# A float32 two-block transformer on one core: head biases on VectorE, the last projection and norm by tokens, finished tiles ahead of weight splits, shorter lags in the convolution stages

## The reference

```
sc = where(allowed, q.k * scale - slope[h] * |i - j|, -inf)      # 8 differential heads, two softmaxes each
z  = q.k * scale                                                  # 8 stick-breaking heads
sc = where(valid, q.k * scale + rel_table[h, clip(i - j)], -inf)  # 8 heads of a band of chunks
x  = x + y @ w_o
g  = causal_dwconv(rmsnorm(x) @ w_gate);  u = rmsnorm(x) @ w_up
x  = x + (silu(g) * u) @ w_down
out = x * rsqrt(mean(x * x) + 1e-6) * final_norm
```

## Time and profile before

| | |
|---|---|
| median of three runs | 2740.82 us |
| profiled execution, its own time | 2740.66 us |
| its span | 2738.8 us |
| TensorE busy / VectorE / ScalarE / GpSimd | 99% / 72% / 47% / 3% |
| DMA: read and written, mean rate, share of its queue for the weights | 499 MB, 182 GB/s, 54.8% |
| weight split on ScalarE / on VectorE, mean | 1.056 / 1.234 us, 929 each |
| chain that ended last, TensorE's share | 95% |

### The profile page before, as it was taken

How to read it: one execution, slowest core, us unless ns; L and a number is a source line. 1 busy time by engine, 2 the same in 40 slices (tenths; PEclk the granted TensorE clock), 3 DMA queues, 4 the chain that set the end, 5 groups by cost and what they waited for, 6 DMA issues and landing times.

```text
span 2738.8 us, 38092 instructions
## 1 busy us (share of the span) xinstructions
PE 2711.5 (99%) x15646; PEld 2356.6 (86%) x15646; DVE 1960.4 (72%) x2399; ACT 1291.2 (47%) x1648; POOL 95.0 (3%) x69
## 2 busy tenths in 40 slices
PE   8999999999999999999999999999999999999997
PEld 7888888888898888888888888888888888888886
DVE  7777888876768665666566885776787757775775
ACT  5444456754545443444344554545544433443444
POOL 1000000011101000000000110000100000000001
PEclk9999999999999999999999999999999999999999
DMA  6555554446555556555555555454555655565553
GB/s 240 191 185 185 178 169 168 145 160 223 181 169 191 186 190 195 191 189 190 192 184 192 193 182 172 148 168 143 166 184 185 201 191 178 196 196 190 185 194 123
DMA packets 138189, 499.01 MB, mean 182 GB/s; under 512 B 15248, under 2 KB 16280, under 8 KB 137888
## 3 DMA queue, kind: packets, MB, share of 16 engines
q1 hardware_dynamic: 136224, 491.67, 54.8%
q10 hardware_dynamic: 1792, 4.91, 0.5%
HBM read 494.41 MB, written 2.11 MB: 181 GB/s over the span
## 4 chain that ended last, share of the span: by engine, by line
PE 95%; DVE 3%; ACT 1%; issue 0%; POOL 0%; DMA 0%; DVEq 0%; ACTq 0%; POOLq 0%
PE PS L484 95%; DVE wlo L1243 1%; ACT whi L833 0%; DVE XG L1445 0%; DVE AR L1253 0%; POOL AR L1755 0%; DMA XG<-in_x 0%; DVE XG L1694 0%; DVE XG L1226 0%; DVE AR L1565 0%; PE PS L576 0%; DVE AR L1629 0%; DVE AR L1250 0%; DVE AR L1226 0%; PE PS L730 0%
## 5 line engine op out<-in xcount | busy, mean ns | idle before, releaser
L484 PE MATMUL PS<-H,whi 128*128 128x512 f32 x5072 | 1785.0, 397 | 9.6 <-DVE wlo L1722 7.8
L1243 DVE TENSOR_TENSOR wlo<-raw,whi 128x1024 fp32r<-128x1024 f32 x929 | 1129.9, 1234 | 625.3 <-ACT whi L833 621.6
L484 PE MATMUL PS<-H,wlo 128*128 128x256 f32 x5072 | 1418.5, 280 | 0.0
L833 ACT ACTIVATE whi<-raw 128x1024 fp32r<-128x1024 f32 x929 | 968.2, 1056 | 896.3 <-PE PS L484 857.8
L484 PEld LDWEIGHTS PS<-H,whi 128*128 128x128 f32 x5072 | 953.7, 188 | 233.9 <-issue 8.0
L484 PEld LDWEIGHTS PS<-H,wlo 128*128 128x128 f32 x5072 | 959.1, 189 | 3.7 <-issue 3.3
L484 PE MATMUL PS<-Y,whi 128*128 128x512 f32 (+1 forms) x2112 | 717.3, 388 | 1.1 <-DVE XG L1694 0.8
L484 PE MATMUL PS<-Y,wlo 128*128 128x256 f32 x2048 | 572.1, 279 | 0.0
L484 PEld LDWEIGHTS PS<-Y,whi 128*128 128x128 f32 x2112 | 392.3, 188 | 87.3 <-DVE XG L1694 2.0
L484 PEld LDWEIGHTS PS<-Y,wlo 128*128 128x128 f32 x2048 | 386.7, 189 | 0.5 <-issue 0.2
L1565 DVE TENSOR_REDUCE AR<-PS 128x512 f32<-128x1024 f32 x140 | 171.6, 1225 | 14.6
(11 more groups left out here) (175 smaller groups left out, 905.4 us busy)
## 6 DMA issues: line engine op xcount, KB each, us to landing
raw<-in_ffn SPq DMA_DIRECT2D x528, 512.0 KB, 3.9
raw<-in_w_in SPq DMA_DIRECT2D x177, 512.0 KB, 4.6
raw<-in_w_qkv SPq DMA_DIRECT2D x96, 512.0 KB, 3.7
raw<-in_w_out SPq DMA_DIRECT2D x64, 512.0 KB, 4.5
raw<-in_w_o SPq DMA_DIRECT2D x40, 512.0 KB, 3.7
raw<-in_w_q SPq DMA_DIRECT2D x8, 512.0 KB, 4.6
raw<-in_w_k SPq DMA_DIRECT2D x8, 512.0 KB, 3.8
raw<-in_w_v SPq DMA_DIRECT2D x8, 512.0 KB, 4.5
```

Of the source, the lines that this page charges most:

```text
L484: return e.matmul(out, l, r, start=start, stop=stop)
L833: a.then_inc(e.activation(c.whi[:, s % NW, :], c.raw[:, s % NRAW, :], ACT.Copy), "whi")
L1243: v.then_inc(e.tensor_tensor(c.wlo[:, s % NW, :], c.raw[:, s % NRAW, :], c.whi[:, s % NW, :].bitcast(F32), ALU.subtract), "wlo")
```

## The change

- d10, d11, d12 become WIDE with m=4: four tiles instead of eight, activations stationary, output by tokens into XT. To have the residual by tokens, new side programs `xt(j)` transpose X after each ao2 tile (TensorE), ScalarE copies. VectorE adds each finished tile in one instruction of 128x1024. The weights of these stages are laid out anew on the host. HELD, which puts off the last two k of a first tile, no longer names these stages.
- In the last tile the last eight k are run for the first half of the tokens, then for the second. The norm is a sum along the row: squares with an accumulator, a reduce over four columns, root on one column. Gains for tiles 0 to 2 are multiplied in beforehand, from a row copy (fgain, 1 MB). Four transfers per token half write the output.
- Biases: VectorE reads scores from PSUM, adds the distances times the slope, or the table rows, writes the negative to SBUF and takes the min along the row in one instruction (tensor_tensor_reduce); ScalarE's Exp reads that with scale -1. The matmuls with c.Dr, J and c.MCr are dropped. Table rows are written to DRAM 128 times each, in eight transfers nine slots apart, so that the later gather needs no flip.
- VectorE takes up tiles before its split of the slot, and ScalarE the value tiles (wv, va, vb, vc). The other steps of ScalarE stay behind its split.
- bc and xs: gather lag 2 to 1, silu lag 6 and 7 to 5, dt's gather lag 3 to 1 and its program two slots sooner; TensorE's `cb` and `xs` idle 6 slots instead of 8.

The diff, cut to its core:

```
-WIDE = ("wv", "va", "vb", "vc")
+VALUES = ("wv", "va", "vb", "vc")
+WIDE = VALUES + ("d10", "d11", "d12")
-HELD = ("wq", "g0", "qa", "g1", "d00", "d01", "d02", "d10", "d11", "d12")
+HELD = ("wq", "g0", "qa", "g1", "d00", "d01", "d02")
+LAST = ("d12", 3)
...
-    out += [(after("bc"), "cb", 0), (after("dt") + 3, "dt", 0)]
+    out += [(after("bc"), "cb", 0), (after("dt") + 1, "dt", 0)]
+    out += [(END[NUM["ao2", j]] // 4 + 2, "xt", j) for j in range(8)]
-LAG = {"bc": 6, "xs": 7, "z": 3, "g0": 1, "g1": 1, "wo2": 2, "xo": 2, "d02": 2, "ao2": 2}
+LAG = {"bc": 5, "xs": 5, "z": 3, "g0": 1, "g1": 1, "wo2": 2, "xo": 2, "d02": 2, "ao2": 2, "d12": 2}
-GATHER_LAG.update(bc=2, xs=2, dt=3)
+GATHER_LAG.update(bc=1, xs=1, dt=1)
...
# tensor_program, dfa(h)
-        for bank in banks:
-            mm(bank[:, 0:384], c.Ir, c.Dr, True, False)
...
# tensor_program, bnd(i)
-            mm(bank[:, 0:128], J, hk[:, 128:256], True, False)
-            mm(bank[:, 128:384], J, hk, False, False)
...
-            p.then_inc(mm(ends, c.Ir, c.MCr.unsqueeze(1).to_broadcast([P, 2, 64]), False, True), "bnd_s")
...
# tensor_program
+    def xt(j):
+        bank = take("xt", j, "b")
+        p.wait_ge(*done("ao2", j))
+        for t in range(2):
+            for i in range(2):
+                last = e.transpose(bank[:, t * T + i * P:t * T + (i + 1) * P], c.xt(2 * j + i)[:, t * P:(t + 1) * P], c.ident)
+        p.then_inc(last, "xt_turn")
...
+            begin, both_halves = b, K - 8 if (stage, j) == LAST else K
+            order = [(k, t) for k in range(both_halves) for t in range(2)]
+            order += [(k, t) for t in range(2) for k in range(both_halves, K)]
...
# vector_program, dfa(h); bnd(i) alike, with its table rows
-                v.then_inc(e.tensor_reduce(st[:, 2 * n + i:2 * n + i + 1], bank[:, o:o + w], AX, ALU.max, negate=True))
-            v.wait_ge(*v.at)
-            v.then_inc(e.tensor_scalar(st[:, 2 * n:2 * n + 2], st[:, 2 * n:2 * n + 2], SLOPES[h], None, ALU.mult), "dif_max")
+                v.then_inc(e.tensor_tensor_reduce(Pb[:, o:o + w], bank[:, o:o + w], c.dist[:, o:o + w], -SLOPES[h], 3e38,
+                                                  ALU.add, ALU.min, st[:, 2 * n + i:2 * n + i + 1]), "dif_max" if i else None)
...
# scalar_program, const: the table rows
-        e.dma_start(c.rows, g8).then_inc(c.sems["rows"], 16)
+        for h in range(8):
+            e.dma_start(c.rows[h:h + 1], g8[h:h + 1, 0:384].unsqueeze(1).to_broadcast([1, P, 384])).then_inc(c.sems["rows"], 16)
+            yield from idle(8)
...
# vector_program, the loop over slots (scalar_program alike for VALUES alone)
         side.step(t)
+        for stage, j in leave_at.get(t, ()):
+            leave(stage, j)
         if t % 2:
             split(t // 2 + NW)
-        for stage, j in leave_at.get(t, ()):
-            leave(stage, j)
...
# vector_program, the end
+    for t in range(2):
+        x2, x3 = c.XT[:, c.tok(t, 2)], c.XT[:, c.tok(t, 3)]
+        m, r, u = (c.fst[:, i + t:i + t + 1] for i in (8, 10, 12))
...
+        v.then_inc(e.tensor_tensor(x3, x3, c.acc[b][:, t, :], ALU.add), "last_x")
+        v.wait_ge("fsq", 7 + t)
+        v.then_inc(e.tensor_reduce(m, c.fst[:, 4 * t:4 * t + 4], AX, ALU.add))
+        v.wait_ge(*v.at)
+        v.then_inc(e.tensor_scalar(m, m, 1.0 / 2048, c.col("eps6"), ALU.mult, ALU.add), "fin_mean")
+        newton(r, m, u, "fin_root", t + 1, "fin_ok")
+        v.wait_ge(*v.at)
+        v.then_inc(e.scalar_tensor_tensor(x3, x3, r, c.fgain[:, 1536:2048], ALU.mult, ALU.mult), "gain_x")
+        v.then_inc(e.tensor_scalar(x2, x2, r, None, ALU.mult), "gain_x")
# scalar_program, the end
+    for t in range(2):
+        a.wait_ge("last_x", t + 1)
+        final_square(3, t)
+        r = c.fst[:, 10 + t:11 + t]
+        refine(r, c.fst[:, 8 + t:9 + t], "fin_mean", t + 1, "fin_root")
+        a.wait_ge("fin_gain", 6)
+        a.wait_ge("fin_ok", t + 1)
+        for j in range(2):
+            a.then_inc(e.activation(c.XT[:, c.tok(t, j)], c.XT[:, c.tok(t, j)], ACT.Copy, scale=r), "scaled")
+        a.wait_ge(*a.at)
+        e.dma_start(c.out[:, c.tok(t, 1)], c.XT[:, c.tok(t, 1)]).then_inc(c.sems["out"], 16)
```

More of the change, by code:

```diff
@@ L101, in gemm_tiles @@
                 out += [(f"g{f}", j, "H", 0, 16, 2), (f"u{f}", j, "H", 0, 16, 2)]
-            out += [(f"d{f}{part}", j, "Y", 0, a1 - a0, 2) for j in range(8)]
+            out += [(f"d{f}{part}", j, "Y", 0, a1 - a0, 4 if f else 2) for j in range(4 if f else 8)]
     return out
@@ L503, in norm @@
             p.wait_ge("c1", 16)
[L504 to L514, removed]
+        p.wait_ge("sum_add", 7 * n + 7)
+        p.then_inc(mm(bank, c.ones, c.SUM, True, True), "norm_sum")
         yield
@@ L538, in cb @@
     def cb(_):
-        yield from idle(8)
+        yield from idle(6)
         p.wait_ge("xbc_silu", 4)
@@ L855, in norm @@
         _, r = norm_dst(c, n)
-        yield from idle(3 if n == 6 else 2)
+        yield from idle(2)
         refine(r, c.SUM[:, 0:T], "norm_mean", n + 1, "norm_root")
@@ L894, in cb @@
     def cb(_):
-        yield from idle(9)
+        yield from idle(7)
         for g in range(4):
@@ L1538, in bnd @@
         P0, P1, q = c.bnd[i]
-        yield from idle(3)
-        for n in range(2):
-            st, bank = c.SM[:, 96 + 16 * (2 * i + n):112 + 16 * (2 * i + n)], c.bank("bnd", i, f"s{n}")
+        yield from idle(2)
+        if i == 0:
+            v.wait_ge("bias", 16)
+            ends = c.BIAS.rearrange("p (h n) -> p h n", h=8)[0:64, :, 192:256]
+            v.then_inc(e.tensor_scalar(ends, ends, NEG, None, ALU.min), "masked")
+        yield
+        for n, Pb in enumerate((P0, P1)):
+            st, bank = c.SM[:, 96 + 16 * (2 * i + n):112 + 16 * (2 * i + n)], c.bank("bnd", i, f"s{n}")
+            bias = c.BIAS[:, (2 * i + n) * T:(2 * i + n + 1) * T]
+            v.wait_ge("masked", 1)
+            if i:
+                v.wait_ge("y_made", made("ao", 8 + i))
+            else:
+                v.wait_ge("dif_pv", 8)
             v.wait_ge("bnd_s", 2 * i + n + 1)
             for o, w, k in ((0, 128, 0), (128, 256, 1)):
-                v.then_inc(e.tensor_reduce(st[:, k:k + 1], bank[:, o:o + w], AX, ALU.max, negate=True), "bnd_max" if k else None)
+                v.then_inc(e.tensor_tensor_reduce(Pb[:, o:o + w], bank[:, o:o + w], bias[:, 256 - w:256], -1.0, 3e38,
+                                                  ALU.add, ALU.min, st[:, k:k + 1]), "bnd_max" if k else None)
         yield from idle(4)
@@ L1696, in follow @@
     def follow(stage, j):
+        if stage == "d12" and j < 3:
+            v.wait_ge("fgain", 16)
+            v.wait_ge("fsq", 2 * j + 2)
+            for t in range(2):
+                x = c.XT[:, c.tok(t, j)]
+                v.then_inc(e.tensor_tensor(x, x, c.fgain[:, j * 512:(j + 1) * 512], ALU.mult), "fin_gain")
         if stage in NEXT:
@@ L1788, in gpsimd_program @@
         for stage, j in leave_at.get(t, ()):
-            if stage in NORM and 0 < j < (7 if stage == "d12" else 8):
+            if stage in NORM and j:
                 add(NORM[stage], j)
         side.step(t)
-    g.wait_ge("norm_ok", 7)
-    g.wait_ge("scaled", 16)
-    for i in (6, 7):
-        x = two(c.xt(2 * i, 2))
-        g.then_inc(e.tensor_tensor(x, x, both(c.RN), ALU.mult), "pool_x")
 def build(nc, d, out):
@@ L1851, in ffn_units @@
         out += pairs(None if part else f"g{f}", gate[:, a0 * P:a1 * P], up[:, a0 * P:a1 * P])
-        out.append(tiles(down[a0 * P:a1 * P], f"d{f}{part}"))
+        rows = down[a0 * P:a1 * P]
+        out.append(wide(rows, 4) if f else tiles(rows, f"d{f}{part}"))
     return units(*out)
```

211 lines of the change are left out of this document (110 added, 101 removed).

## The result

The kernel after takes **2727.17 us** (median of 5 runs, 2727.01 to 2727.36) against 2740.53 us (5 runs, 2740.14 to 2741.65): a ratio of 0.9951, with a 95% interval of 0.9936 to 0.9965. It is 0.5% faster, and a ratio of 1 lies outside the interval; but it gained 13.4 us where 24.5 were forecast. The time lies inside the stated range of 2710 to 2728, and outside the range of 2710 to 2722 that the prediction gave its own case.

The account below looks back on a forecast made before the run. TensorE, busy 99% of the span, was taken as the bound. Terms of -4.7, -2.8, -6.4, +3.5, -0.9, -6.8 and -6.4 summed to -24.5 us, taking 2740.66 to 2716 us; stated range 2710 to 2728.

Parts of the forecast that it names:

- its own case: Whole kernel: all counted savings and costs arrive, giving 2716 us, range 2710 to 2722; chance 73%.
- rival A: Heads, bands, xs: waits fill the shortened slots, 9.2 us come back, 2725 us, or 2728 with two lags; chance 15%.
- Part 1: d10 to d12: wide token-major tiles cost 0.340 us a block against 0.346, over 704 blocks: -4.7 us.
- rival D: d10 to d12: weight loads are exposed, so a quarter fewer save 67 us instead of 4.7: 2654 us; chance 2%.
- Part 2: Differential heads and band pairs: moving biases to VectorE cuts TensorE's stream by 2.8 and 6.4 us.
- Part 3: After ao2 tiles: eight visits transposing the residual add 3.5 us; dropping the last norm's matmuls saves 0.9.
- Part 4: sb, dt, xs, wv, xo: finished tiles before splits and shorter lags remove TensorE waits: -6.8 us.
- rival B: Up tiles and first projection: late weight splits starve TensorE, 51 us lost, 2767 us; chance 5%.
- Part 5: Behind the last block: the closing chain and transfers take 8.8 us instead of 15.2: -6.4 us.
- C: Wide tiles run at the pair's pace, reordering has no effect, heads wait: 2737 us; chance 5%.

Follow-up runs that it names:

- e7: Kernel after plus single transposes behind d10 and in z, and float32 products of 256 columns behind d11 and in wo2, some pairs into the tile: 2721.58 us.
- e6: Kernel after with the lags, bank order, idle slots and dt program start of the kernel before in dt, bc and xs: 2726.07 us.
- e3: Kernel after with VectorE's adds of xo tiles behind its weight split again: 2727.13 us, single run.
- e4: Kernel after with ScalarE's take-up of value tiles behind its split again: 2727.40 us, single run.
- e2: Kernel before plus one visit of four constant transposes ahead of the g1 tile behind d10: 2750.40 us against 2740.63.
- e5: Kernel before plus a series of spare transposes and products of various kinds between and within g1 and u1 tiles: 2768.16 us, single run.
- e8: Kernel after with old dt, bc, xs lags, value tiles behind ScalarE's split, and float32 products behind d10, d11, in ka and wo2: 2720.64 us.
- e1: Kernel after plus one float32 product of 256 columns at the start of the g1 tiles behind d10 and d11: 2728.10 us.

## Why the prediction came out as it did

**The number.** The stated range held 2727.17 only because it was stretched to rival A's 2728. A's mechanism gave 1.07 of its 9.2 us; the rest of the miss came from elsewhere. That the time fell inside the range was luck, and the case that was given 73% missed by 5 us.

**Part 1, last projection by tokens: right as a term, wrong in its surroundings.** The 704 blocks gained 4.7 us, and the triple took its 0.680. What failed is the step that took 0.346 us a block as the price of every narrow pair, from one stretch of g0. The pace is a state, and behind four of the five token-major stages that narrow pairs follow it was the slow one (ka before; g1 behind d10 and d11 after), in every trace. Its price, +5.9 us, is more than the part's gain; with the resets of e7 5.3 of them came back. The rule on loads, rival D, which would have given 2654, did not apply: a triple with one load fewer for two blocks saves 6.7 ns a block, not 0.5 x 189. The Trainium skill (TensorE: Matmul & The Clock Gate, section "The mechanism") has the rule that a load overlaps a running matmul only when the row group differs; the trace of after disagrees again, with loads of 0.189 us beside pairs of 0.347. The same section also lets a load run ahead of matmuls in flight into the background weight buffer, which the prediction left out and these rows do not contradict.

**Part 2, biases: right.** -2.8 and -6.1 for -2.8 and -6.4. The operation that the trace of before lacked stands in the groups by line and shape of the kernel after:

```profile
L1494 DVE CUSTOM_DVE_ANT_0 AR<-PS,CR 128x256 f32<-128x256 f32 x16 | 6.7, 421 | 0.0
...
L1494 DVE DVE_READ_ACCUMULATOR2_ANT AR<- 128x1 f32 x32 | 2.7, 84 | 0.0
```

421 ns for 256 columns where the max took 415, as taken, and 84 for reading the result.

**Part 3, transposes of the residual: right, +3.5 by the visits.** The same missed state added 0.85 between them, alike in all seven traces that have these visits.

**Part 4, order and lags: half.** dt and z were right by size, but e6 shows that the lags had no part in it, or a negative one: the prediction had put the 1.9 us of the last xs pair down to lag 5. The 3.3 us of xo and wv's values fell to 0.8. The step that failed is the one in which the adds of xo come earlier at no cost: it counted VectorE 3.2 us of work a tile against 2.9 for TensorE, concluded that banks and buffers just hold that, and did not ask who is next to need VectorE. It is H for g0's first tile (e3). Likewise the split behind vb's values was called covered, from TensorE's view of the weights; the head's weights, queued behind VectorE's split, are due sooner (e4, 1.07 us). Before sb's first tile the wait for the gather became one of 0.7 us for the split behind it: rival B's mechanism, at one place and small.

**Part 5, the end: right.** -7.0 from the add on for -6.4. The chain of small operations was 4.3 us for 4.4, the transfers 3.9 for 4.3. The start's 0.5 was not foreseen; in the profiled executions of all versions the first matmul came at 7.3 to 7.8 us, so most of it may be scatter.

**The rivals.** A named the measured level (2725 to 2728), but not by its mechanism: of 9.2 us cut from heads and bands only 1.07 was waited for. B stayed small: behind the start TensorE's waits on splits are 0.7 us in all, at sb's first tile. C's pace argument was wrong for the wide tiles themselves. No rival held a change of pace in untouched stages, though its trace was at hand.

Adding up: -24.5, +6.8 of slow pace (5.95 + 0.85), +2.5 in xo and g0, +1.1 at kb, +0.6 in xs and z, +0.5 at sb, +0.3 in the bands, -0.6 at the end and -0.5 at the start: -13.8, against -13.7 measured between the spans.

## What to carry to other kernels

Take the price of a plain step from several stretches of the trace, one behind each kind of neighbour that the change makes, before it is multiplied by hundreds: 2% in a pace of TensorE outweighed the part that it followed, and one spare product behind each of two stages gave most of it back. Where the pace comes out slow can differ between executions of the same code, so look at more than one trace. Where work is put first on an engine that has more to do than TensorE in that stretch, look for the next consumer behind the stretch; the wait moves there. Undo each tuning of lags by itself: here one of them cost what another brought.

## What was not expected of the hardware

- A stream of fp32r pairs (a 512- and a 256-column pass, weights loaded for each) has two stable paces at the same granted clock of 1.00: 0.3467 and 0.3533 us a pair. Neither has a wait or a lower busy share; the count of matmuls in a window of fixed length shows it (233 or 228 in 40 us). It lasts: 1,344 pairs in e2.
- Visits of 0.1 to 0.9 us switch it in both directions. In e2 and e5 four transposes gave the slow pace each time, a single float32 product of 256 or 512 columns in the run of pairs the fast one (seven events in e5, two in e7, four in e8), directly behind a token-major stage not (e1). Other kinds were irregular.
- None of this is a strict rule. Over all ten traces four transposes left the slow pace 151 times of 152 (the exception is in e8's xs), and a single float32 product of 256 columns behind slow pairs left the fast one 125 times of 127 (both exceptions in e2's ao1). The 512-column product of a norm at qa's start left 95 slow pairs behind fast ones in after, e4 and e8, and fast ones in the other seven. In after and e1 the code up to there is the same. The cause was not found.
- Token-major triples of 512-column passes took 0.680 us in va, d10, d11 and d12 alike; in vb and vc, where visits stand between them, no own pace was read.
